# A two-layer hybrid encoder: norm sums on VectorE, first experts in two halves, and another end for the last token group

## The reference

```python
def rmsnorm(x, g):
    y = xf * lax.rsqrt(jnp.mean(xf * xf, axis=-1, keepdims=True) + EPS) * g
for i in range(DEPTH):
    y = rmsnorm(h, mix_norm_g[i])
    h = h + (mixer_ab(y, ...) if i % 2 == 0 else mixer_conformer(y, ...))
    y = rmsnorm(h, ffn_norm_g[i])
    h = h + peer(y, peer_w_q[i], peer_sub_keys[i], peer_u[i], peer_v[i])
h = rmsnorm(h, final_norm_g)
return h[:, N_META:N_META + S, :]

def peer(y, w_q, sub_keys, u, v):
    s = einsum('thpc,pnc->thpn', (yt @ w_q).reshape(T, 8, 2, 128), sub_keys)
    val, idx = top_k(s, 16); cand = val[:, :, 0, :, None] + val[:, :, 1, None, :]
    top_val, top_pos = top_k(cand.reshape(T, 8, 256), 16)      # -> expert rows
    act = softmax(top_val) * gelu(einsum('thkd,td->thk', u[expert], yt))
    return einsum('thk,thkd->td', act, v[expert])
```

## Time and profile before

| | us |
|---|---|
| median of 3 runs | 1607.42 (1606.4 to 1611.76) |
| the profiled execution, its own time | 1606.77 |
| its span | 1605.0 |
| PE busy | 1046.8 (65%) |
| DVE busy | 1111.9 (69%) |
| ACT busy | 461.3 (29%) |
| POOL busy | 500.8 (31%) |
| moved by DMA | 646.70 MB, mean 403 GB/s |

### The profile page before, as it was taken

One profiled execution on the slowest core, in us unless ns is written; L12 is line 12 of the kernel. 1 busy time (PEld: TensorE's weight loads), 2 busy tenths in 40 slices (PEclk: granted clock), 3 DMA queues, 4 the chain that ended last, 5 costly groups with the idle time before them and its releaser, 6 DMA issues.

```text
span 1605.0 us, 19986 instructions
## 1 busy us (share of the span) xinstructions
PE 1046.8 (65%) x6936; PEld 711.0 (44%) x6936; DVE 1111.9 (69%) x3119; ACT 461.3 (29%) x953; POOL 500.8 (31%) x541
## 2 busy tenths in 40 slices
PE   8997876757734577778574477877576444544454
PEld 8995642525511266656362155665263111211111
DVE  3436878676457776997756777987765777777764
ACT  4111553111111345742111335743222111111110
POOL 0003333333223333332322323332332333333330
PEclk9998877867955699888796589877788555555666
DMA  9979999999999999999999999999999999999994
GB/s 369 408 259 402 374 420 421 417 421 420 416 420 420 421 378 415 420 415 394 422 416 420 421 411 403 417 405 374 420 418 419 421 422 421 421 421 423 420 420 190
DMA packets 105300, 646.70 MB, mean 403 GB/s; under 512 B 11632, under 2 KB 15728, under 8 KB 37616
## 3 DMA queue, kind: packets, MB, share of 16 engines
q0 software_dynamic: 76032, 553.68, 83.5%
q1 hardware_dynamic: 25536, 89.66, 14.2%
q10 hardware_dynamic: 3632, 2.08, 0.4%
HBM read 644.33 MB, written 1.05 MB: 402 GB/s over the span
## 4 chain that ended last, share of the span: by engine, by line
DMA 40%; PE 28%; DVE 15%; POOL 5%; issue 5%; ACT 4%; DVEq 2%; POOLq 0%; ACTq 0%
DMA ring<-in_uv_dram,expert 36%; PE ps L691 14%; DVE ring L1221 7%; PE ps L868 7%; POOL ring L406 5%; DMA wring<-in_wall_dram 5%; PE ps L881 2%; DVE side L1276 2%; PE ps L698 1%; PE ps L909 1%; ACT side L590 1%; PE ps L856 1%; ACT yg L471 1%; ACT osb L651 1%; ACT L475 0%
## 5 line engine op out<-in xcount | busy, mean ns | idle before, releaser
L1221 DVE CUSTOM_DVE_ANT_0 ring<-ring,ps 128x1024 f32<-128x1024 f32 x528 | 634.8, 1217 | 314.9 <-DMA ring<-in_uv_dram,expert 261.2
L406 POOL DMA_INDIRECT ring<-in_uv_dram,expert x528 | 498.7, 945 | 1068.8 <-PE ps L868 808.2
L868 PE MATMUL ps<-ring,mix 128*32 128x512 f32 x2112 | 369.3, 834 | 327.3 <-DVE mix L1237 327.3
L868 PEld LDWEIGHTS ps<-ring,mix 128*32 128x32 f32 x2112 | 67.8, 135 | 531.7 <-DVE mix L1237 391.0
L665 ACT ACTIVATE gel<-dots 128x4 f32<-128x4 f32 x132 | 27.1, 205 | 761.7 <-DVE dots L1221 761.4
L691 PE MATMUL ps<-yT,wring 128*128 128x128 f32 (+1 forms) x1184 | 159.6, 294 | 48.2 <-DMA wring<-in_wall_dram 27.6
L691 PEld LDWEIGHTS ps<-yT,wring 128*128 128x128 f32 x1184 | 150.7, 202 | 63.6 <-DMA wring<-in_wall_dram 34.2
L881 PE MATMUL ps<-sel,osb 128*128 128x16 f32 x528 | 84.1, 304 | 70.6 <-ACT osb L651 70.6
L881 PEld LDWEIGHTS ps<-sel,osb 128*128 128x128 f32 x528 | 80.7, 241 | 108.9 <-ACT osb L651 108.9
L590 ACT ACTIVATE side<-ident,params 128x128 f32<-128x128 f32 x310 | 96.3, 389 | 15.6 <-PE ps L909 14.8
L856 PE MATMUL ps<-ident,yg 128*128 128x128 f32 x264 | 48.0, 342 | 58.0 <-DVE dots L1221 58.0
(11 more groups left out here) (211 smaller groups left out, 1135.5 us busy)
## 6 DMA issues: line engine op xcount, KB each, us to landing
wring<-in_wall_dram SPq DMA_DIRECT2D x102, 512.0 KB, 11.8
ring<-in_wall_dram SPq DMA_DIRECT2D x44, 512.0 KB, 14.5
kept<-in_wall_dram SPq DMA_DIRECT2D x24, 512.0 KB, 17.0
ring<-in_uv_dram,expert POOLq DMA_INDIRECT x528, 16.1
out_dram<-fo ACTq DMA_DIRECT2D x16, 64.0 KB, 6.7
hT<-in_xT_dram ACTq DMA_DIRECT2D x1, 576.0 KB, 15.9
hT<-in_xT_dram SPq DMA_DIRECT2D x2, 256.0 KB, 3.2
params<-in_smalls_dram ACTq DMA_DIRECT2D x1, 380.0 KB, 17.7
```

The source lines that it names most:

```text
L406: pool.indirect_dma_start(out=ring[:, i % R, :], out_offset=None, in_=uv, in_offset=bass.IndirectOffsetOnAxis(ap=expert[:, n % 2, k:k + 1] ...
L868: mm = pe.matmul(po[32 * j:32 * j + 32, half, :], mix[:, k, :], ring[:, slot, D + 512 * half:D + 512 * (half + 1)], start=(q == 0), stop=( ...
L1221: nc.vector.tensor_tensor_reduce(out=row, in0=row, in1=yrep, scale=1.0, scalar=0.0, op0=ALU.mult, op1=ALU.add, accum_out=dots[:, k:k + 1]) ...
```

## The change

Five edits. (1) PE no longer sums squares with 8 matmuls: DVE adds the 8 channel blocks with one reduction (tokens 0 to 127, `s_sum`; tokens 128 to 271, `s_sumx`), or block by block (`add_square`) beside `outA`, and one matmul with `ones` sums the partitions. The first of these matmuls now stands behind the first chunk. Eight matmuls of `ones` with `ones`, whose result is not used, stand at PE's start. (2) ACT loads the Sqrt table ahead of the sum, and issues the transfers of the other tokens and of the remaining parameters behind the root instead of ahead of it. (3) The query weights are ordered by key set; the scores of group 0 against the first set are made behind chunk 9 of `qA` and searched by DVE behind chunk 11. (4) The experts of group 0 are made in two halves of 8 ranks; POOL starts after the first. (5) The last group: ranks 12 to 14 are weighted and summed ahead of rank 15, whose gather is the last; the copy, the sum over the heads and the norm go by halves of 512 channels, on token rows instead of transposed, with the old rows transposed onto the same PSUM banks before (`last_rows`); the gain comes in as a new input of 16 rows; SP stores the group before and one half, ACT the other.

```diff
+            pool.wait_ge(s_half, 1)
             for n in range(N):
-                pool.wait_ge(s_idx, n + 1)
                 for k in range(TOPK):
+                    if k == 0 and n or k == 8 and n == 0:
+                        pool.wait_ge(s_idx, n + 1)
...
+            act.wait_ge(s_const, 6)
+            act.activation(warm[:, :], epsc[:, :], ACT.Sqrt)
+            act.wait_ge(s_ss, 1)
+            act.activation(rstd[:, 0:TA], ps[:, 7, 0:TA], ACT.Sqrt, bias=epsc[:, :], scale=1.0 / D).then_inc(s_rms, 1)
             act.dma_start(hT[:, :, TA:L], xT[:, C * TA:C * L].rearrange("p (c t) -> p c t", t=TB)).then_inc(s_x[2], 16)
             act.dma_start(params[:, PAR["conv"]:NPAR], smalls[:, PAR["conv"]:NPAR]).then_inc(s_par2, 16)
-            act.wait_ge(s_const, 6)
-            act.wait_ge(s_ss, 1)
-            act.activation(rstd[:, 0:TA], ps[:, 7, 0:TA], ACT.Sqrt, bias=epsc[:, :], scale=1.0 / D).then_inc(s_rms, 1)
             act.wait_ge(s_x[2], 16)
             act.activation(sqB0[:, :, :], hT[:, :, TA:L], ACT.Square).then_inc(s_sqx, 1)
...
+            act.activation(warm[:, :], epsc[:, :], ACT.Gelu)
+            for ks in (slice(12, 15), slice(15, 16)):
+                act.wait_ge(s_dot, TOPK * (N - 1) + ks.stop)
+                act.activation(gel[:, ks], dots[:, ks], ACT.Gelu).then_inc(s_gel, 1)
+            act.activation(warm[:, :], epsc[:, :], ACT.Sqrt)
+            act.wait_ge(s_ot, N - 1)
...
+            act.copy(osb[:, 0:D // 2], po[:, 0, :]).then_inc(s_oh[0], 1)
...
+            act.wait_ge(s_zr, 1)
+            act.activation(junk[:, 0, :], zr[:, 0, :], ACT.Square, accum_out=ssq[:, 0:1]).then_inc(s_zs, 1)
+            act.wait_ge(s_zs, 1)
...
+            act.wait_ge(s_zr, 2)
+            act.activation(junk[:, 1, :], zr[:, 1, :], ACT.Square, accum_out=ssq[:, 1:2]).then_inc(s_zs, 1)
+            act.wait_ge(s_zs, 3)
+            act.activation(root[:, :], ssq[:, 1:2], ACT.Sqrt, bias=base[:, :], scale=1.0 / D).then_inc(s_root, 1)
+            act.wait_ge(s_zg, 2)
+            act.wait_ge(s_rinv, 1)
+            act.activation(zg[:, 1, :], zg[:, 1, :], ACT.Copy, scale=rinv[:, :]).then_inc(s_zf[1], 1)
...
             pe.wait_ge(s_const, 6)
-            for c in range(C):
-                pe.wait_ge(s_sq, 2 * c // C + 1)
-                last = pe.matmul(ps[:, 7, 0:TA], ones[:, :], sq[:, c, :], start=(c == 0), stop=(c == C - 1))
-            last.then_inc(s_ss, 1)
+            for _ in range(8):
+                pe.matmul(ps[:, 6, 0:P], ones[:, :], ones[:, :], start=True, stop=True)
             for k in range(24):
                 if k == 0:
                     pe.wait_ge(s_hg, C)
                 chunk("inA", k, lambda c: yT[:, c, 0:TA], TA)
+                if k == 0:
+                    pe.wait_ge(s_sum, 1)
+                    pe.matmul(ps[:, 7, 0:TA], ones[:, :], rs[:, 0:TA], start=True, stop=True).then_inc(s_ss, 1)
...
-            pe.wait_ge(s_sqx, 1)
+            pe.wait_ge(s_sumx, 1)
             pe.wait_ge(s_ze, 2)
-            for c in range(C):
-                last = pe.matmul(ps[:, 3, 0:TB], ones[:, :], sqB0[:, c, :], start=(c == 0), stop=(c == C - 1))
-            last.then_inc(s_ssx, 1)
...
+            pe.matmul(ps[:, 3, 0:TB], ones[:, :], xs[:, 0:TB], start=True, stop=True).then_inc(s_ssx, 1)
...
             pe.wait_ge(s_b, AC)
             for k in range(C):
                 chunk("outA", k, lambda c: mixT[:, c, 0:TA], TA)
-                if k >= 2:
-                    second_sums(k - 2)
...
             for k in range(16):
@@ -770,8 +823,14 @@
                     pe.wait_ge(s_hg2, C)
                 chunk("qA", k, lambda c: hg2[:, c, :], TA)
                 if k == 0:
-                    second_sums(C - 2)
-                    second_sums(C - 1)
+                    pe.wait_ge(s_sum, 2)
+                    pe.matmul(ps[:, 7, 0:TA], ones[:, :], rs[:, 0:TA], start=True, stop=True).then_inc(s_ss, 1)
+                if k == 9:
+                    evacuated(pe, "qA", 6)
+                    evacuated(pe, "qA", 7)
+                    pe.wait_ge(s_par2, 16)
+                    score(0, 0).then_inc(s_sc0, 1)
...
-                for s in range(2):
-                    last = pe.matmul(psc[:, s * NK:(s + 1) * NK], qT[:, s, query(n), :, :].rearrange("p h t -> p (h t)"),
-                                     keysT[:, 2 * layer_of(n) + s, :], start=True, stop=True)
+                for s in range(2) if n else (1,):
+                    last = score(n, s)
                 last.then_inc(s_sc, 1)
...
+            def last_rows():
+                evacuated(pe, "q11", 14)
+                evacuated(pe, "q11", 15)
+                pe.wait_ge(s_rb, 2 * C)
+                for c in range(C):
+                    pe.matmul(zr[:, c // 4, c % 4 * P:(c % 4 + 1) * P], hT[:, c, tokens(N - 1)], ident[:, :],
+                              start=(c % 4 == 0), stop=False)
...
-            values(N - 1, 3)
-            back(N - 1)
-            final_sums(N - 1)
+            last_rows()
+            for part, js in enumerate((range(3), range(3, 4))):
+                pe.wait_ge(s_m, 4 * N + part)
+                for half in range(2):
+                    for j in js:
+                        slot = (N * TOPK - 4 + j) % R
+                        mm = pe.matmul(po[32 * j:32 * j + 32, half, :], mix[:, TOPK - 4 + j, :],
+                                       ring[:, slot, D + 512 * half:D + 512 * (half + 1)], start=False, stop=True)
+                    if part == 1:
+                        mm.then_inc(s_vh, 1)
+            for half in range(2):
+                pe.wait_ge(s_oh[half], 1)
+                pe.matmul(zr[:, half, :], sel4[:, :], osb[:, half * D // 2:(half + 1) * D // 2], start=False, stop=True
+                          ).then_inc(s_zr, 1)
...
+            dve.wait_ge(s_sq, 2)
+            nc.vector.tensor_reduce(out=rs[:, 0:TA], in_=sq[:, :, :].rearrange("p c t -> p t c"), axis=AX, op=ALU.add
+                                    ).then_inc(s_sum, 1)
...
+            def best_half(s, ready):
+                dve.wait_ge(ready, 1)
+                nc.vector.max(val[:, s, 0:8], sc[s])
+                dve.drain()
+                nc.vector.max_index(idx[:, s, 0:8], val[:, s, 0:8], sc[s])
+                last = nc.vector.match_replace(rest[:, s, :], val[:, s, 0:8], sc[s], LOW)
+                if s == 1:
+                    last.then_inc(s_psc, 1)
+                dve.drain()
+                nc.vector.max(val[:, s, 8:16], rest[:, s, :])
+            def route_first():
+                spare = rest[:, :, :].rearrange("p s (k j) -> p s k j", j=TOPK)
+                best_pairs(0)
+                dve.drain()
+                nc.vector.max_index(topp[:, 0:8], topv[:, 0:8], c1)
+                rows_of(0, slice(0, 8), spare).then_inc(s_half, 1)
+                nc.vector.match_replace(c2, topv[:, 0:8], c1, LOW)
+                nc.vector.tensor_scalar(negm[:, :], topv[:, 0:1], -1.0, None, ALU.mult)
+                dve.drain()
+                nc.vector.max(topv[:, 8:16], c2).then_inc(s_top, 1)
+                dve.drain()
+                nc.vector.max_index(topp[:, 8:16], topv[:, 8:16], c2)
+                rows_of(0, slice(8, 16), spare).then_inc(s_idx, 1)
...
+            def rows_of(n, ks, hot):
+                count = ks.stop - ks.start
+                dve.drain()
+                nc.vector.tensor_scalar(posu[:, 0, ks], topp[:, ks], 4, None, ALU.logical_shift_right)
+                nc.vector.tensor_scalar(posu[:, 1, ks], topp[:, ks], 15, None, ALU.bitwise_and)
+                dve.drain()
+                nc.vector.tensor_copy(posf[:, :, ks], posu[:, :, ks])
...
+                nc.vector.tensor_reduce(out=picked[:, :, ks], in_=hot[:, :, :, :], axis=AX, op=ALU.add)
+                dve.drain()
+                return nc.vector.tensor_tensor(expert[:, n % 2, ks], picked[:, 0, ks], picked[:, 1, ks], ALU.add)
...
+                if k == 4:
+                    dve.wait_ge(s_sqx, 1)
+                    nc.vector.tensor_reduce(out=xs[:, 0:TB], in_=sqB0[:, :, :].rearrange("p c t -> p t c"), axis=AX, op=ALU.add
+                                            ).then_inc(s_sumx, 1)
...
+            def add_square(c):
+                dve.wait_ge(s_sq2, c + 1)
+                if c > 1:
+                    dve.wait_ge(s_add, c - 1)
+                return nc.vector.tensor_tensor(rs[:, 0:TA], sq[:, 0, :] if c == 1 else rs[:, 0:TA], sq[:, c, :], ALU.add)
...
                 nc.vector.tensor_scalar(hg2[:, c, :], hv, par("ffn_g", c), None, ALU.mult).then_inc(s_hg2, 1)
+                if c >= 2:
+                    add_square(c - 1).then_inc(s_add, 1)
...
+            add_square(C - 1).then_inc(s_sum, 1)
...
-                nc.vector.tensor_tensor(qT[:, k % 2, 0:GF, k // 2, :],
+                nc.vector.tensor_tensor(qT[:, k // H, 0:GF, k % H, :],
                                         ps[:, m % 2, 0:TA].rearrange("p (g t) -> p g t", t=GT),
```

(21 more changed lines are left out.)

188 lines of the change are left out of this document (108 added, 80 removed).

## The result

| | before | changed |
|---|---|---|
| median of 12 runs each, one chip | 1607.89 | 1615.08 (1611.5 to 1617.17) |
| ratio, 95% interval | | 1.0040 [1.0031, 1.0049] |
| the profiled execution, its own time | 1606.77 | 1614.31 |
| its span | 1605.0 | 1612.2 |

What follows compares the result with a forecast made beforehand. One long stream of gathers, with PE's chain before it and an engine-after-engine end, bounds the kernel. 1606.77 + 5.4 (start) - 3.7 (end) = 1608.5, with 0.65 for the median 1609.1 us; range 1602 to 1613.5.

Steps and rivals of the forecast that it cites:

- the start: PE's chain to the end of the first 16 `inB` chunks: 5.4 us later at 138.4, and so at 191.
- The landing: ACT's 576 KB transfer of the other tokens: issued at 9.8, taking 15.9 us, landed at 25.7.
- The reduction: DVE's reduction of the squares of tokens 128 to 271, between its fifth and sixth chunk: 1.27 us, ceiling 1.37.
- The clock behind the stop: PE from chunk 7 on: one chunk at the low clock, 2.0 us more, with nothing and 3.9 as ends.
- The sums saved: PE's sums of squares before the first chunk, the second sums and those beside `outA`: together 3.05 us saved.
- The bound: Start's loss: 0.5 us if the transfer needed only 11 us; 9.3 with slow first chunk and two behind the stop.
- case B: Rival: PE slow already in chunk 0, longer stop at chunk 7; start costs 9.3, end gives 2.7: 1614.0, chance 0.20.
- The first gathers: From scores' end to first gather: 3.4 us less, and 0.3 of the scores; first gather about 117, worth nothing.
- case D: Rival: the start's loss is hidden by a DMA queue full until 190, only the end counts: 1603.7, chance 0.14.
- case C: Rival: the 576 KB land by 18.6, no stop; start 3.6 earlier, end 3.7: 1600.1, chance 0.14.
- The end: Last landing to last store: 3.7 us saved, between 2.7 and 5.3 (PE at high clock); last dot to store 9 to 11.

Runs made afterwards that it cites:

- e7: The changed kernel with three contiguous additions instead of the one reduction over a transposed view: 1627.58 us, ratio 1.0070 to the kernel before.
- e12: The changed kernel as it is, run again: 1614.15 us, ratio 1.0040 to the kernel before.
- e14: The changed kernel with the old end: 1624.87 us, ratio 1.0040 to the kernel before.
- e16: The changed kernel as it is, run again on a slower chip: 1622.35 us, ratio 1.0038 to the kernel before.
- e18: The changed kernel with the old end, run again: 1626.14 us, ratio 1.0062 to the kernel before.
- e4: The changed kernel with 36 unused matmuls ahead of chunk 7 of `inA`: 1610.46 us, ratio 1.0021 to the kernel before.
- e6: The changed kernel with transfers ahead of the root, reduction behind chunk 20, and POOL waiting for all 16 ranks: 1612.80 us, ratio 0.9981 to the kernel before.
- e9: The changed kernel with transfers ahead of the root, reduction behind chunk 20, and ranks 12 to 15 weighted and summed together: 1604.88 us, ratio 0.9983.
- e1: The changed kernel with the transfers ahead of the root again, reduction still behind chunk 4: 1605.11 us, ratio 0.9983 to the kernel before.
- e3: The changed kernel with the transfers ahead of the root again and the reduction behind chunk 20: 1602.60 us, ratio 0.9966 to the kernel before.
- e15: The changed kernel with three contiguous additions instead of the one reduction, run again: 1625.72 us, ratio 1.0056 to the kernel before.
- e2: The changed kernel with the reduction behind chunk 20 instead of chunk 4, transfers still late: 1607.02 us, ratio 0.9994 to the kernel before.
- e10: The changed kernel with transfers ahead of the root, reduction behind chunk 20, and 14 unused matmuls instead of 8 at PE's start: 1611.83 us, ratio 0.9979.
- e13: The kernel before with the new end alone, run again: 1614.60 us, ratio 0.9968 to the kernel before.

## Why the prediction was wrong

The mechanism of the forecast came true link by link; the sum failed first in the start, "6.5 + 2.0 - 3.05 = 5.4 us later at 138.4". It was 9.4. For the two profiled executions the forecast was 5.4 - 3.7 = 1.7 us and they are 7.5 apart. Of the 5.8 between, 4.0 are the start; the end gave 1.7 more than forecast, the other way; and 3.5 came in stretches that the sum had at nothing.

- **The landing.** Predicted 25.7, measured 27.34: chunk 0 began 0.3 later and took 2.02 instead of 1.8, so the issue was at 10.3 and not at 9.8, and the transfer took 17.0 us instead of 15.9. This gives 1.6 of the error.
- **The reduction.** I took 1.27 with 1.37 as the ceiling, and it took 2.09: 0.8 of the error, and outside my bounds. The ceiling of 1.37 was too low even by the reduction in the earlier trace rows: 0.69 for 512 elements makes 1.55 for 1152. Both rows are of instructions that read their elements in a row, and this one reads a transposed view. The trace of before had two such instructions (L976 and L978, 0.36 and 0.25 us), and the changed kernel has them still:

```profile
7.48 0.36 DVE L1057 TENSOR_REDUCE sel<-ident 128x16 f32<-128x128 f32 x1
7.75 0.25 DVE L1059 TENSOR_REDUCE sel<-ident 128x16 f32<-128x64 f32 x1
```

  64 elements more cost 0.11 us, 1.7 ns each; 1152 of them make 2.1. No run reduced the same elements read in a row, so that the view is the cause is argued from these rows. I looked for the nearest row by size and operation and not by the way it reads.
- **The clock behind the stop.** 3.2 us (8.53 - 5.36) instead of 2.0; inside the ends of nothing and 3.9 that I had given. In the six other profiles with the stop (e7, e12, e14 to e16, e18) the three chunks took 7.05 to 8.27 us, so the clock cost 1.7 to 2.9 there, and the 2.0 was within what executions show. e4 shows that it is the clock and that the idle time causes it. The row that I had read for it, 0.73 in the earlier trace rows, was a weak one: PE idles again within that stretch, and the 16 instructions behind the stop of 3.48 us took 3.35 in before, but 1.92 in the changed kernel.
- **The sums saved.** With chunk 7 at 30.99 instead of 22.0 (+9.0) and the clock (+3.2), the 9.4 leaves 2.8 saved, against 3.05.
- **The bound.** "If it needed only 11 us" was the side that I looked at. On the other side my own case B (a slow chunk 0, then issue and landing 2 us later) had 0.20. Chunk 0 took 3.04 to 3.75 us in ten of the 14 profiles with eight unused matmuls, so this case is the common one, and the changed kernel's own profiled execution the luckiest. B's time, 1614.0, came within 1.1 us, with a start of its size (9.3), but that is in part luck: in that profile chunk 0 was fast, and it was the landing, the reduction and the clock; and B had only 2.7 us for the end.
- **The first gathers.** From the scores' end (115.12) to the first gather 6.8 us, against 9.66: 2.9 saved, predicted 3.7. That it is worth nothing was right (e6). Gather 28 was late by the start's whole loss and 1.0 more, so case D is out; case C (no stop) is out by the row of 8.85 us. In the eight profiles with halves on the two faster chips the way from the end of `inB` to that gather is 0.4 to 1.8 us longer than before (52.7); why is open.
- **The end.** Predicted 9 to 11 us from the last dot to the last store, measured 8.13; 5.4 saved instead of 3.7. PE stayed at the high clock, the other of the two cases that I had worked out (5.3), for which "9 to 11" left no room. In e9, the one profile without the split of the ranks, it had the low clock; in the 15 with it, it never had. Timed alone the new end gave 3.9 on average, near my 3.7, but for another reason than mine: it is the old end that takes 11.9 or 13.5 us, not the new one that varies.

The terms of the two profiled executions make 9.4 - 5.4 = 4.0 of their 7.5 us. Of the rest 0.3 is the last dot, 0.3 the time around the span, 0.1 behind the last store, 1.0 the stretch ahead of gather 28. Some 1.7 us between that gather and the last dot stay unexplained, and a single profile can't explain them: this stretch differs by 3 us between the two profiles of the changed kernel on the faster chips, and in e1 it is 7.1 us longer than in before, in an execution 4.1 us above its median.

The best version is e3: the change without its late transfers and with the reduction behind chunk 20, at 0.9966 [0.9952, 0.9979] and 0.9978 [0.9964, 0.9992] of the time before.

## What to carry to other kernels

A wait that is put into an in-order engine's stream stalls what stands behind it, and through the bank that this engine empties, PE: before a transfer is issued later, look for the earliest instruction behind which its data are now awaited. When such a stop can't be avoided, count the clock behind it as well, or keep PE busy with work that is thrown away. Price an instruction by the row that reads its data in the same pattern, not by the one of the same size.

## What the runs showed of the hardware

- A float32 reduction over a transposed view took 2.09 us for 1152 elements a partition and 1.87 for 1024 (changed kernel); three additions of rows (576, 288, 144 elements: 0.76, 0.46, 0.31) did the same work in 1.6 (e7, e15).
- After 8.85 us without a matmul the granted clock was 0.55 over 8 us; with 0.51 us (e1) and 1.19 us (e2) of waiting three and two chunks ran at the full clock.
- Chunk 0, behind eight unused matmuls and 1.6 to 2.7 us of idle PE, took anything from 2.02 to 3.75 us for the same 16 instructions, from one execution to the next. The longer wait did not make the slower chunk: 2.02 came after 2.13 us, 3.60 after 1.60 (e18).
- The first values' 16 instructions, after a wait of 3.48 us in every profile, took 1.92 us in five of them (the changed kernel, e10 to e13) and 2.96 to 3.64 in 13 others.
- The five chips gave the kernel before medians of 1607.6 and 1607.8, and of 1615.5, 1617.9 and 1618.5 us. Only on the three slower ones does the profile have waits put down to "remote", up to 5.5 us at a time (e6).
